# Two gathered tiles of rows in place of a combining pass that waits for the last two expert blocks

## The chip, the cores and the metric

One core of a Trainium2 chip runs the whole program once. The metric is the device time of one execution in microseconds; the kernel before has a median of 1506.51 us over 3 runs.

## The reference, cut to what matters

One decoder layer runs over 1056 tokens (1024 of a prompt and 32 of samples) of width 1024: a mixing sub-layer, then a mixture of 32 experts of which each token takes two, then a final RMSNorm. Only the end matters here:

```
h = x + mix
# expert e of token t, k = 0, 1:  silu(hn W_gate[e]) * (hn W_up[e]) W_down[e]
h[t] = h[t] + gate[t, 0] * out[t, 0] + gate[t, 1] * out[t, 1]
y = rms_norm(h, norm_final_w)
```

The reference sorts the 2112 assignments of a token to an expert by expert and pads them to blocks of 128 rows. With the given inputs no expert gets more than 110 rows, so there are 32 blocks, one for each expert. Block 30 holds 61 rows that are in use and block 31 holds 73; 121 tokens have a row in one of these two blocks, 13 of them in both.

## The kernel before, in words

The program is written engine by engine, and each engine runs its own list in the order in which it is written; semaphores join them. After the front part (projections, mixing, router) comes `experts`, and then `combine`, a block of its own that no engine enters before all have left `experts`.

**Experts.** Blocks are numbered 0 to 31. For each, POOL gathers the block's rows of the normalised input by an indirect DMA (`gather`, L1822 to L1828, tile `xg`), PE turns them (L1859), and ACT and DVE split all float32 operands into a high and a low part (`wgu_h` L1928, `wgu_l` L2048, `wd_h` L1934, `wd_l` L2057, `xh_blk` L1939, `xl_blk` L2052), so that PE makes each product of three matmuls (L62 to L64). SP loads the weights: four pieces of `wgu` (1 MB each, L1785) and four of `wd` (0.5 MB each, L1792) for each block, each as soon as DVE has read the piece before. The result of a block is copied by DVE to `yb` (`unload_y`, L2042) and POOL scatters its rows by an indirect DMA to the scratch tensor `picked` in HBM (`scatter`, L1830 to L1836). `picked` has 2112 rows: row t is the first expert's result of token t, row 1056 + t the second's. Rows of a block that are not in use have an index out of bounds and are not moved. Block 31 is different: its result goes to the tile `xg`, and POOL scatters it from there (L1846 to L1850). The last blocks stand behind the loops: `m` is 30 on SP, PE, ACT and DVE, and 29 on POOL.

At the end of its list for the experts SP loads the final norm's weights `w_final` (L1801), the residual rows of tiles 0 to 3 (`h_final`, L1804) and of tiles 4 to 8 (`h_late`, L1807), and then waits until all 32 scatters have landed:

```
            sp.wait_ge(y_stored, m * 16 + 32)
```

**Combine.** Tiles 0 to 7 are 128 tokens each and tile 8 is the 32 sample tokens. SP loads for each tile both rows of `picked` of each token (`yy`, 1 MB a tile, L2126). Tiles 8, 0, 2, 4 and 6 are summed by DVE (`add`, two SCALAR_TENSOR_TENSOR, L2186), tiles 1, 3, 5 and 7 by PE with matrices `diag` that hold the gates (L2148 to L2150). ACT takes the mean square and its root (L2165 to L2172), DVE takes the reciprocal and scales (`norm`, L2196 to L2204), and POOL stores the tile (L2134). The order is 8, 0, 1, ..., 7.

## Time and profile before

| | |
|---|---|
| median of 3 runs | 1506.51 us (1503.09 to 1506.59) |
| the profiled execution, its own time | 1505.11 us |
| its span in the trace | 1503.4 us |
| PE busy | 1416.1 us (94%) |
| DVE busy | 1061.5 us (71%) |
| ACT busy | 766.1 us (51%) |
| POOL busy | 568.4 us (38%) |
| data moved by the DMA engines | 361.07 MB |

The span begins with the first instruction and ends with the last; 1.7 us of the execution's own time lie outside of it. A busy share is an average over the whole program, in which the experts take from about 863 to 1464 us and combining from there to the end. In the profile's rows of waits, the time is what an engine sat idle before the instruction named, and behind the arrow stands what ended it.

### The profile page before, as it was taken

The page shows a single profiled execution, that of the slowest core. Times are in us where ns is not written, and L with a number is a line of the kernel's source. Part 1 is how long each engine was busy: PE and PEld are TensorE (multiplying, and loading weights), DVE is VectorE, ACT ScalarE, POOL GpSimd, SP SyncE. Part 2 cuts the span into 40 slices and gives each one's busy share as a digit, 9 for nine tenths or more (in the row PEclk, how much of TensorE's full clock was granted, in tenths as well). Part 3 has the DMA queues.
Part 4 walks back from the last instruction along what each step waited for, and adds up shares of the span by engine and source line. Part 5 has one row for each costly group of instructions (what it writes and reads, how often), then busy time and mean ns, then how long its engine had stood idle before and what let it go on. Part 6 is the DMA issues. An engine that isn't in the chain of part 4 may idle for free. (4 is left out here: it accounts for less than half of the span.)

```text
span 1503.4 us, 21686 instructions
## 1 busy us (share of the span) xinstructions
PE 1416.1 (94%) x7625; PEld 1233.0 (82%) x7625; DVE 1061.5 (71%) x1225; ACT 766.1 (51%) x891; POOL 568.4 (38%) x345
## 2 busy tenths in 40 slices
PE   6999999999999999899999659999999999999976
PEld 5999999999999998788877548888888888888852
DVE  6687722366666664545463579999999999999956
ACT  6332222333333335344433438777777777777734
POOL 2323324454444442485644014333433333333311
PEclk9999999999999999999999669999999999999997
DMA  5222333234444445876653659999999999999958
GB/s 197 65 78 86 126 95 111 80 130 143 144 141 147 138 144 167 294 219 239 209 168 130 231 201 383 402 396 390 377 381 362 389 379 383 385 388 387 369 211 343
DMA packets 115793, 361.07 MB, mean 240 GB/s; under 512 B 18772, under 2 KB 48468, under 8 KB 99348
## 3 DMA queue, kind: packets, MB, share of 16 engines
q1 hardware_dynamic: 100164, 322.37, 58.6%
q0 software_dynamic: 15568, 37.87, 7.3%
q8 instruction: 41, 0.67, 0.2%
q14 instruction: 20, 0.16, 0.0%
HBM read 316.52 MB, written 59.64 MB: 250 GB/s over the span
## 5 line engine op out<-in xcount | busy, mean ns | idle before, releaser
L2048 DVE TENSOR_TENSOR wgu_l<-wgu,wgu_h 128x2048 fp32r<-128x2048 f32 x128 | 290.0, 2288 | 27.4 <-ACT wgu_h L1928 26.5
L1928 ACT CAST wgu_h<-wgu 128x2048 fp32r<-128x2048 f32 x124 | 237.4, 1915 | 100.6 <-PE bank0and L64 100.5
L62 PE MATMUL bank0and<-wgu_h,xh_blk 128*128 128x512 f32 x512 | 203.7, 398 | 2.9 <-DVE xl_blk L2052 2.9
L64 PE MATMUL bank0and<-wgu_h,xl_blk 128*128 128x512 f32 x512 | 200.9, 392 | 0.0
L62 PE MATMUL bank0and<-xh,wh 128*128 128x352 f32 x576 | 197.6, 343 | 3.0 <-ACT raw L906 3.0
L63 PE MATMUL bank0and<-wgu_l,xh_blk 128*128 128x512 f32 x512 | 200.3, 391 | 0.0
L64 PE MATMUL bank0and<-xh,wl 128*128 128x352 f32 x576 | 186.7, 324 | 0.0
L63 PE MATMUL bank0and<-xl,wh 128*128 128x352 f32 x576 | 186.5, 324 | 0.0
L1671 POOL TENSOR_TENSOR wol<-wo,woh 128x1024 fp32r<-128x1024 f32 x48 | 121.4, 2536 | 123.5 <-ACT woh L996 123.5
L1835 POOL DMA_INDIRECT scratch_picked<-yb,dst x31 | 92.7, 2991 | 197.5 <-DVE yb L2042 197.5
L2057 DVE TENSOR_TENSOR wd_l<-wd,wd_h 128x1024 fp32r<-128x1024 f32 x128 | 148.2, 1219 | 1.2 <-ACT wd_h L1934 1.0
L1622 POOL TENSOR_TENSOR wl<-w,wh 128x1024 fp32r<-128x1024 f32 x36 | 87.7, 2437 | 155.7 <-ACT wh L893 155.7
L1934 ACT CAST wd_h<-wd 128x1024 fp32r<-128x1024 f32 x128 | 124.9, 1049 | 1.7 <-PE bank2and L64 1.7
L62 PEld LDWEIGHTS bank0and<-wgu_h,xh_blk 128*128 128x128 f32 x512 | 96.8, 189 | 22.7 <-issue 2.8
L62 PEld LDWEIGHTS bank0and<-xh,wh 128*128 128x128 f32 x576 | 109.7, 190 | 6.9 <-issue 5.6
L64 PEld LDWEIGHTS bank0and<-wgu_h,xl_blk 128*128 128x128 f32 x512 | 96.6, 189 | 20.8
L63 PEld LDWEIGHTS bank0and<-wgu_l,xh_blk 128*128 128x128 f32 x512 | 96.9, 189 | 19.4
L63 PEld LDWEIGHTS bank0and<-xl,wh 128*128 128x128 f32 x576 | 110.0, 191 | 2.6 <-issue 1.9
L64 PEld LDWEIGHTS bank0and<-xh,wl 128*128 128x128 f32 x576 | 109.3, 190 | 0.0
L1191 DVE COPY stage<-bank2and 128x512 f32<-128x512 f32 x26 | 18.0, 692 | 123.3 <-PE bank2and L568 123.3
L915 ACT ACTIVATE feat<-bank0and 128x352 f32<-128x352 f32 x48 | 22.1, 463 | 156.1 <-PE bank0and L64 156.0
L62 PE MATMUL bank2and<-wd_h,hT_h 128*128 128x512 f32 x248 | 99.3, 401 | 0.0
(496 smaller groups left out, 3234.5 us busy)
## 6 DMA issues: line engine op xcount, KB each, us to landing
wgu<-in_w_gate_up SPq DMA_DIRECT2D x128, 1024.0 KB, 7.6
wd<-in_w_down SPq DMA_DIRECT2D x128, 512.0 KB, 7.6
wo<-in_w_out SPq DMA_DIRECT2D x48, 512.0 KB, 4.9
w<-in_w_in_tiles SPq DMA_DIRECT2D x36, 512.0 KB, 3.6
yy<-scratch_picked SPq DMA_DIRECT2D x8, 1024.0 KB, 12.6
scratch_xb<-stage POOLq DMA_DIRECT2D x10, 512.0 KB, 4.0
xb<-scratch_xb SPq DMA_DIRECT2D x8, 640.0 KB, 4.4
scratch_uT<-feat SPq DMA_DIRECT2D x8, 528.0 KB, 5.0
```

What stands on the lines that cost most here:

```text
L62: nc.tensor.matmul(acc, lh, rh, start=start, stop=False)
L63: nc.tensor.matmul(acc, lh, rl, start=False, stop=False)
L64: return nc.tensor.matmul(acc, ll, rh, start=False, stop=stop)
L915: nc.scalar.activation(feat[q % 2][:, b * TB:(b + 1) * TB], bank[b][:, 0:TB], func).then_inc(acc_free, 1)
L1191: ins = nc.vector.tensor_copy(stage[j][:, 4 * g:4 * g + 4, :], bank[3 + g][:].rearrange("p (t c) -> p t c", t=4))
L1622: nc.gpsimd.tensor_tensor(wl[q % 2][:], w[q % 2][:], wh[q % 2][:].bitcast(F32), ALU.subtract).then_inc(w_split, 1)
L1671: nc.gpsimd.tensor_tensor(wol[n % 3][:], wo[n % 3][:], woh[n % 3][:].bitcast(F32), ALU.subtract).then_inc(w_split, 1)
L1835: pool.indirect_dma_start(out=S["picked"], out_offset=bass.IndirectOffsetOnAxis(ap=dst[:], axis=0), in_=yb[:], in_offset=None, bounds_chec ...
L1928: nc.scalar.copy(wgu_h[:, s], wgu[:, s]).then_inc(gu_high, 1)
L1934: nc.scalar.copy(wd_h[:, p, :], wd[:, p, :]).then_inc(down_high, 1)
L2048: nc.vector.tensor_tensor(wgu_l[:, s], wgu[:, s], wgu_h[:, s].bitcast(F32), ALU.subtract).then_inc(gu_split, 1)
L2057: nc.vector.tensor_tensor(wd_l[:, p, :], wd[:, p, :], wd_h[:, p, :].bitcast(F32), ALU.subtract).then_inc(down_split, 1)
```

## The change

The combining pass is moved into the block `experts`, and the function `combine` is gone.

- At the start of the experts SP stores the gates to a new scratch tensor `gates` and, behind the loads of block 1's `wgu`, loads `w_final` and the residual rows of tiles 0 to 3. Tiles 8 and 4 are loaded before the last `wd`, tiles 5, 6 and 7 behind it.
- POOL fills `yb` with zeros and scatters these zeros to the rows of blocks 30 and 31 in `picked`, between its first gathers.
- SP's wait before it loads `yy` has the same number, `m * 16 + 32`, but with the two scatters of zeros it is met when block 29 has been scattered. The nine tiles are then combined with zeros in the place of the rows of blocks 30 and 31, and SP, no longer POOL, stores them whole to one output `y`.
- POOL scatters block 30 only when all nine `yy` have been loaded, then block 31 when block 30 has landed. It then gathers two more tiles, 9 and 10: the residual rows, the gates, and both rows of `picked` of the tokens of block 30 and of block 31. DVE adds and scales them, and POOL scatters them to `y` when all nine stores have landed, tile 10 after tile 9 has landed.
- The tiles on PE are 2, 4, 6 and 7, the order is 8, 1, 0, 2, ..., 7, 9, 10.

```diff
+            for t in range(2):
+                rows, n = ((slice(0, SEQ), P), (slice(SEQ, T), TS))[t]
+                tiles = slice(0, NT) if t == 0 else slice(NT, NT + 1)
+                sp.dma_start(S["gates"][rows, :].rearrange("(t p) k -> p t k", p=n), S["gate"][0:n, tiles, :]).then_inc(loaded[0], 16)
             m = blocks_but_three(sp) + 1
             load_gate_up(1)
+            sp.wait_ge(rows_ready, 1)
+            sp.dma_start(w_final[:], A["norm_final_w"][0].partition_broadcast(P)).then_inc(loaded[0], 16)
+            for t in range(FIRST):
+                sp.dma_start(h[t], S["h"][t * P:t * P + P, :]).then_inc(loaded[t], 16)
...
+            sp.wait_ge(gu_split, m * 4 + 8)
+            sp.sem_inc(holder, 1)
+            load_h(NT)
+            load_h(4)
             load_down(m + 1)
...
+            for t in (5, 6, 7):
+                load_h(t)
+            picked = S["picked"].rearrange("(k t) d -> t k d", k=2)
             sp.wait_ge(y_stored, m * 16 + 32)
-            sp.sem_inc(holder, 1)
+            for t in (8, 1, 0, 2, 3, 4, 5, 6, 7):
+                used = 0 if t == 0 else (t + 1) // 2
+                if used:
+                    sp.wait_ge(gu_used, m * 4 + (4 + used))
+                sp.sem_inc(holder, 1)
+                sp.dma_start(yy[t][0:live(t)], picked[t * P:t * P + live(t)]).then_inc(loaded[t], 16)
+            for n, t in enumerate(ORDER[0:NT + 1]):
+                sp.wait_ge(out_ready, n + 1)
+                sp.dma_start(A["y"][t * P:t * P + live(t), :], h[t][0:live(t), :]).then_inc(out_stored, 16)
+            sp.wait_ge(out_stored, 16 * (NT + 1))
...
             gather(1)
+            for j in range(2):
+                if j:
+                    pool.wait_ge(y_stored, 16)
+                then_own(pool, nc.gpsimd.tensor_copy(dst[:], of_row[:, 1, bass.ds(m + (1 + j), 1)]), dst_ready, j + 1)
+                pool.indirect_dma_start(out=S["picked"], out_offset=bass.IndirectOffsetOnAxis(ap=dst[:], axis=0),
+                                        in_=yb[:], in_offset=None, bounds_check=2 * T - 1, oob_is_err=False).then_inc(y_stored, 16)
             gather(2)
...
+            is_loaded(pool, 0)
...
+            late_gather(0, h[NT + 1], S["h"])
+            for j in range(2):
+                late_gather(j, late_gate[:, j, :], S["gates"])
+            for t in range(NT + 1):
+                is_loaded(pool, t)
             scatter(m + 1)
...
+            pool.wait_ge(y_stored, m * 16 + 64)
             pool.wait_ge(y_done, last + 1)
...
+            pool.wait_ge(y_stored, m * 16 + 80)
+            pool.sem_inc(holder, 1)
+            for k in range(2):
+                late_gather(0, yy[NT + 1][:, k, :], S["picked"], k)
+            late_gather(1, h[NT + 2], S["h"])
+            for k in range(2):
+                late_gather(1, yy[NT + 2][:, k, :], S["picked"], k)
+            pool.wait_ge(out_stored, 16 * (NT + 1))
+            store_late(0)
+            pool.wait_ge(late_stored, 16)
+            store_late(1)
+            pool.wait_ge(late_stored, 32)
...
+            make_diag(0)
+            make_diag(1)
+            gated(m + 1)
+            low_down(m + 1, range(2))
+            low_hid(m + 1, (last_h, last_l))
+            dve.wait_ge(hid_ready, m + 2)
+            make_diag(2)
+            make_diag(3)
+            unload_y(m)
+            low_down(m + 1, range(2, 4))
             add(NT)
+            dve.wait_ge(down_used, (m + 1) * 4 + 4)
+            nc.vector.tensor_copy(xg[:], S["banks45"][:]).then_inc(y_done, 1)
+            add(1)
+            norm(NT)
             add(0)
...
+            norm(6)
+            norm(7)
+            dve.wait_ge(xg_loaded, m * 16 + 160)
+            dve.sem_inc(holder, 1)
+            add(9)
+            add(10)
+            norm(9)
+            norm(10)
```

The helpers that it calls are the ones that stood in `combine`, and these two on POOL:

```
            def late_gather(j, out, table, k=0):
                pool.indirect_dma_start(out=out, out_offset=None, in_=table,
                                        in_offset=bass.IndirectOffsetOnAxis(ap=late_row[:, j, k:k + 1], axis=0),
                                        bounds_check=(2 * T if k else T) - 1, oob_is_err=False).then_inc(xg_loaded, 16)

            def store_late(j):
                pool.wait_ge(out_ready, NT + 2 + j)
                pool.indirect_dma_start(out=A["y"], out_offset=bass.IndirectOffsetOnAxis(ap=late_row[:, j, 0:1], axis=0), in_=h[NT + 1 + j],
                                        in_offset=None, bounds_check=T - 1, oob_is_err=False).then_inc(late_stored, 16)
```

How it moves instructions: first SP at the end of the program, in the kernel before. `yy` with a number is the tile of one t, 10035 for t = 8 and 10027 on for t = 0 on; in square brackets stand the semaphores that the instruction waits for.

```order
L1807 DMA h_late<-scratch_h 128x1024 [waits gu_split]
L1807 DMA h_late<-scratch_h 128x1024 x3
L1807 DMA h_late<-scratch_h 32x1024
L1808 ISA
L1714 UNCONDITIONAL_BRANCH [waits y_stored]
L2122 UNCONDITIONAL_BRANCH [waits barrier_Pool_Activation_PE_DVE_SP_release]
L2126 DMA yy_10035<-scratch_picked 32x2x1024
L2126 DMA yy_10028<-scratch_picked 128x2x1024
L2126 DMA yy_10027<-scratch_picked 128x2x1024
```

The same place of the changed kernel, where `yy_8914` on are the tiles 0 on:

```order
L1844 DMA h_rest<-scratch_h 128x1024 x3
L1854 ISA
L1860 DMA yy_8922<-scratch_picked 32x2x1024 [waits y_stored,gu_used]
...
L1860 DMA yy_8920<-scratch_picked 128x2x1024 [waits gu_used]
L1860 DMA yy_8921<-scratch_picked 128x2x1024 [waits gu_used]
L1863 DMA out_y<-h_rest 32x1024 [waits out_ready]
L1863 DMA out_y<-h_first 128x1024 [waits out_ready] x4
L1863 DMA out_y<-h_rest 128x1024 [waits out_ready] x4
L1714 UNCONDITIONAL_BRANCH [waits out_stored]
```

The barrier between the two blocks is gone, the loads of `yy` follow a wait for `y_stored` directly, and the stores stand on SP's queue behind the loads.

POOL at the end of the program, in the kernel before:

```order
L1835 DMA scratch_picked<-yb,dst 2112x1024 [waits dst_ready,y_done]
L1846 ISA
L1846 COPY src<-of_row 128x1
L52 REGISTER_ALU
L1849 DMA scratch_picked<-xg,src 2112x1024 [waits dst_ready,y_done]
L1714 UNCONDITIONAL_BRANCH
L2128 UNCONDITIONAL_BRANCH [waits barrier_Pool_Activation_PE_DVE_SP_gather]
L2134 DMA out_y_sample<-h_late 32x1024 [waits out_ready]
```

And in the changed kernel, from block 30's scatter on:

```order
L1887 ISA [waits final_loaded5,final_loaded4,final_loaded6,final_loaded3,final_loaded7,final_loaded2,final_loaded1,final_loaded0]
L1889 COPY dst<-of_row 128x1 [waits y_stored]
L52 REGISTER_ALU
L1892 DMA scratch_picked<-yb,dst 2112x1024 [waits dst_ready,y_done]
...
L1938 DMA scratch_picked<-xg,src 2112x1024 [waits y_stored,y_done]
L1941 REGISTER_ALU [waits down_split]
L1917 DMA wd<-scratch_picked,late_row 128x1024 [waits y_stored]
L1917 DMA wd<-scratch_picked,late_row 128x1024
L1917 DMA xg<-scratch_h,late_row 128x1024
L1917 DMA wd<-scratch_picked,late_row 128x1024 x2
L1923 DMA out_y<-wgu,late_row 1056x1024 [waits out_ready,out_stored]
L1923 DMA out_y<-xg,late_row 1056x1024 [waits out_ready,late_stored]
```

Block 30's scatter has moved behind all loads of `yy`, and behind it stand five waits for a DMA one after the other: block 30's scatter, block 31's, the gathers (for which DVE waits), tile 9's store and tile 10's.

## Rows read from the trace of the kernel before

**Rows 1.** The page: span, and PE's busy time and share of the span

```profile
span 1503.4 us, 21686 instructions
PE 1416.1 (94%) x7625; PEld 1233.0 (82%) x7625; DVE 1061.5 (71%) x1225; ACT 766.1 (51%) x891; POOL 568.4 (38%) x345
```

**Rows 2.** Windows: stretch, its length, busy time by engine, TensorE's clock, DMA share, GB/s

```profile
900.00:1400.00 500.00, 498.88 (x2365) 414.90 (x2366) 480.30 (x340) 382.10 (x314) 181.81 (x112) 1.00 0.99 385
1440.35:1447.88 7.53, 7.53 (x37) 6.26 (x36) 1.61 (x2) 2.30 (x3) 0.00 (x2) 1.00 0.92 360
1458.05:1461.20 3.15, 0.00 (x0) 0.00 (x0) 0.00 (x0) 0.00 (x0) 0.97 (x1) 0.62 0.24 95
1470.50:1478.19 7.69, 7.57 (x12) 3.32 (x13) 6.52 (x6) 4.63 (x9) 0.52 (x1) 0.65 1.03 413
```

**Rows 3.** Timeline of SP's queue: start, us, line, issue, count

```profile
1434.14 3.71 SPq L1792 DMA_DIRECT2D wd<-in_w_down  x4
1437.90 0.98 SPq L1801 DMA_DIRECT2D w_final<-in_norm_final_w  x1
1441.21 2.77 SPq L1807 DMA_DIRECT2D h_late<-scratch_h  x5
1464.55 8.21 SPq L2126 DMA_DIRECT2D yy<-scratch_picked  x9
```

**Rows 4.** Timeline of POOL at the end; in square brackets idle before and its end

```profile
1439.36 0.99 POOL L1835 DMA_INDIRECT scratch_picked<-yb,dst  x1 [10.05 <-DVE yb L2042]
1447.88 0.34 POOL L1832 COPY dst<-of_row 128x1 int32 x1 [7.53 <-DMA scratch_picked<-yb,dst]
1458.05 0.97 POOL L1849 DMA_INDIRECT scratch_picked<-xg,src  x1 [4.10 <-DVE xg L2088]
1499.12 0.53 POOL L2134 DMA_DIRECT2D out_y_prompt<-h_late  x1 [0.99 <-DVE h_late L2200]
```

**Rows 5.** SP's waits from 1400 us on: the one for the scatters

```profile
SPq L1809 <- DMA scratch_picked<-xg,src: 17.2, 1, 17.2
```

**Rows 6.** Timeline of DVE while combining

```profile
1470.51 2.58 DVE L2186 SCALAR_TENSOR_TENSOR h_late<-yy,gate,h_late 32x1024 f32<-32x1024 f32 x2 [4.24 <-DMA yy<-scratch_picked]
1478.19 2.60 DVE L2186 SCALAR_TENSOR_TENSOR h_final<-yy,gate,h_final 128x1024 f32<-128x1024 f32 x2 [0.83 <-DMA yy<-scratch_picked]
1490.40 2.60 DVE L2186 SCALAR_TENSOR_TENSOR h_late<-yy,gate,h_late 128x1024 f32<-128x1024 f32 x2 [1.26 <-DMA yy<-scratch_picked]
1492.92 0.16 DVE L2196 RECIPROCAL st_f<-st_f 128x1 f32<-128x1 f32 x1
1493.11 1.29 DVE L2203 SCALAR_TENSOR_TENSOR h_late<-h_late,st_f,w_final 128x1024 f32<-128x1024 f32 x1
```

**Rows 7.** Timeline of SP, ACT and POOL at the start of the experts

```profile
878.21 26.15 SPq L1785 DMA_DIRECT2D wgu<-in_w_gate_up  x8
905.71 5.77 ACT L1928 CAST wgu_h<-wgu 128x2048 fp32r<-128x2048 f32 x3
882.89 1.05 POOL L1826 DMA_INDIRECT xg<-scratch_hn,src  x1 [2.64 <-PE bank4and L1859]
899.38 1.01 POOL L1826 DMA_INDIRECT xg<-scratch_hn,src  x1 [5.54 <-PE bank4and L1859]
```

**Rows 8.** Timeline of POOL: the first gather, then a scatter in the loop

```profile
875.59 1.11 POOL L1816 DMA_INDIRECT xg<-scratch_hn,of_row  x1 [11.57 <-DVE blk_i L2032]
880.05 0.20 POOL L1823 COPY src<-of_row 128x1 int32<-128x1 int32 x1 [3.35 <-DMA xg<-scratch_hn,of_row]
...
1209.10 2.83 POOL L1835 DMA_INDIRECT scratch_picked<-yb,dst  x1 [9.32 <-DVE yb L2042]
1218.77 1.53 POOL L1832 COPY dst<-of_row 128x1 int32 x1 [1.80 <-DMA scratch_picked<-yb,dst]
```

**Rows 9.** Timeline of ACT while combining: tile 6's square, sum and root

```profile
1493.03 1.06 ACT L2171 ACTIVATE junkf<-h_late 128x1024 f32<-128x1024 f32 x1 [2.68 <-DVE h_late L2186]
...
1494.22 0.30 ACT L2172 ACTIVATE st_f<-st_f,eps 128x1 f32<-128x1 f32 x1
```

More of the change, by code:

```diff
@@ L1763, in experts, with live, psum_of, is_loaded @@
         y_done, y_stored = sem("y_done"), sem("y_stored")
-        holder = C["holder"]
+        loaded = [sem(f"final_loaded{t}") for t in range(NT)]
+        loaded, loaded_at = loaded + [loaded[1]], [48 + 32, 64, 32, 32, 32, 32, 32, 32, 64]
+        out_stored, late_stored = sem("out_stored"), sem("late_stored")
+        summed, rms, out_ready = (sem(n) for n in ("summed", "rms", "out_ready"))
+        diag_ready, pe_summed = sem("diag_ready"), sem("pe_summed")
+        holder = C["holder"]
+        def live(t):
+            return TS if t == NT else P
+        def psum_of(t, half):
+            return bank[(0, 6, 2, 4)[ON_PE.index(t)] + half][:, :]
+        def is_loaded(eng, t):
+            eng.wait_ge(loaded[t], loaded_at[t])
         block = ctx.enter_context(nc.Block())
@@ L1918, in _ @@
             down(m + 1, first=4)
+            for n, t in enumerate(ON_PE):
+                is_loaded(pe, t)
+                if n == 0:
+                    pe.wait_ge(diag_ready, 8)
+                    pe.wait_ge(hT_done, m + 2)
+                if n >= 2:
+                    pe.wait_ge(y_done, m + (n - 1))
+                for half in range(2):
+                    s = slice(half * 512, (half + 1) * 512)
+                    acc = psum_of(t, half)
+                    nc.tensor.matmul(acc, C["ident"][:], h[t][:, s], start=True, stop=False)
+                    nc.tensor.matmul(acc, diag[n // 2][:, n % 2, 0, :], yy[t][:, 0, s], start=False, stop=False)
+                    nc.tensor.matmul(acc, diag[n // 2][:, n % 2, 1, :], yy[t][:, 1, s], start=False, stop=True).then_inc(pe_summed, 1)
         @block.scalar
@@ L2182, in add, with make_diag @@
+            def make_diag(n):
+                for k in range(2):
+                    nc.vector.tensor_scalar(diag[n // 2][:, n % 2, k, :], C["ident"][:], gate[ON_PE[n]][:, k:k + 1], None, ALU.mult).then_inc(diag_ready, 1)
             def add(t):
-                r = rows_of(t)
-                dve.wait_ge(loaded[t], loaded_at[t])
+                r = live(t)
+                if t <= NT:
+                    is_loaded(dve, t)
                 for k in range(2):
-                    ins = nc.vector.scalar_tensor_tensor(out=h[t][0:r, :], in0=yy[t][0:r, k, :], scalar=S["gate"][0:r, t, k:k + 1],
+                    ins = nc.vector.scalar_tensor_tensor(out=h[t][0:r, :], in0=yy[t][0:r, k, :], scalar=gate[t][0:r, k:k + 1],
@@ L2204, in norm @@
                                                          op0=ALU.mult, op1=ALU.mult)
                 ins.then_inc(out_ready, 1)
-            for n, t in enumerate(ON_PE):
-                for k in range(2):
-                    nc.vector.tensor_scalar(diag[:, n, k, :], C["ident"][:], S["gate"][:, t, k:k + 1], None, ALU.mult).then_inc(diag_ready, 1)
+            make_diag(0)
[3 more added lines that the diff above has]
+            low_hid(m + 1, (last_h, last_l))
@@ L2210, in _ @@
+            dve.wait_ge(hid_ready, m + 2)
[3 more added lines that the diff above has]
+            low_down(m + 1, range(2, 4))
             add(NT)
+            dve.wait_ge(down_used, (m + 1) * 4 + 4)
+            nc.vector.tensor_copy(xg[:], S["banks45"][:]).then_inc(y_done, 1)
+            add(1)
+            norm(NT)
             add(0)
-            norm(NT)
-            for t in range(2, NT, 2):
-                add(t)
-                norm(t - 2)
-                norm(t - 1)
@@ L2217, in _ @@
-            norm(NT - 2)
-            norm(NT - 1)
+            norm(1)
+            norm(0)
+            add(3)
+            norm(2)
+            norm(3)
+            add(5)
+            norm(4)
+            norm(5)
+            norm(6)
[6 more added lines that the diff above has]
+            norm(10)
+FIRST = 4
+ON_PE = [2, 4, 6, 7]
+ON_DVE = [8, 1, 0, 3, 5, 9, 10]
+ORDER = [8, 1, 0, 2, 3, 4, 5, 6, 7, 9, 10]
```

179 lines of the change are left out of this document (68 added, 111 removed).

## The prediction

> **What bounds the kernel now.** I read the windows first, then the queues at the end. In the loop over the experts PE is busy 498.9 of 500 us at the full clock, level 2.4 GHz, with the DMA engines at a share of 0.99 and 385 GB/s [rows 1, 2]. The change takes no matmul out of that loop, so a gain can only come from what follows it. There the timeline of SP is the one to read: the loads of `yy` begin at 1464.55 [rows 3], after SP has waited 17.2 us for block 31's scatter [rows 5]. That scatter starts at 1458.05 on POOL [rows 4]; SP's last issue of residual rows ends at 1443.98 [rows 3], and 17.2 us later is 1461.2. The other 3.3 us are the barrier and the entry into the next block of code. The last `yy` lands at 1490.4, when DVE stops waiting for it [rows 6]. From there 13.0 us of sums, norms and the last stores end the span at 1503.4. So the tail is: wait for the scatters (A), load 8.25 MiB (B), finish (C).
>
> The change starts B earlier, and puts a longer C behind it. I work out both.
>
> **A, when the loads of `yy` start.** SP now waits for block 29's scatter. It starts at 1439.36 and has landed at 1447.88, 7.5 us after its issue ended [rows 4], in a stretch where the DMA engines moved 360 GB/s [rows 2]. A scatter in the loop takes about as long: 1211.9 to 1218.8, 6.8 us [rows 8]. Block 31's scatter, with the DMA engines nearly empty, took 3.15 us from its start (1458.05 to 1461.2) [rows 2, 4]. These are the two prices, 1442.5 and 1447.9. In between lies what is queued on SP: `w_final` and tiles 0 to 3 no longer come here, and 4.3 MB remain (tiles 8 and 4 from 1432.8, `wd` from 1434.1 [rows 3], then tiles 5 to 7). At 413 GB/s [rows 2] these 10.5 us of transfer plus 2 us to the first landing run until about 1445.3. I take 1445.2, nearer to the loaded price because the queue is still full for most of it. There is no barrier any more, so the loads start 19.4 us earlier than at 1464.55.
>
> This is one place where the Trainium skill says otherwise. The trace shows a scatter landing 7.5 us after its issue beside a full queue of SP, against 2.2 us beside an empty one [rows 4]. By "DMA: Bandwidth & Descriptors", section "Queues, rings and completion order", each DMA engine goes round robin between the queues at every packet, so a scatter of 61 rows should hardly wait behind SP's backlog. By that A would be near 1442.5 and the total 2.7 us lower; the rows contradict it.
>
> **B, loading.** Before, tiles 8, 1, 0, 3 and 2 (4.25 MiB) had landed at 1478.19, 13.65 us after the first issue, without any store beside them until 1477.67, and tiles 8 and 1 at 1470.51, after 6.0 us [rows 6]: 3 MiB in 7.7 us, 2.55 us each, the 413 GB/s of that window [rows 2]. All nine thus need 13.65 + 4 x 2.55 = 23.9 us. Tile 9's residual rows are gathered meanwhile (61 rows of 4 KB, 0.6 us of transfer): 24.4 us, against 25.8 before, since the stores now queue behind the loads instead of beside them. All `yy` have landed at 1445.2 + 24.4 = 1469.6.
>
> **C, what follows the last `yy`.** The nine plain tiles are not what ends: DVE is through with the experts by 1458.05 [rows 4], add(8) fits ahead of that, and four adds at 2.60 and nine norms at about 1.5 [rows 6] make 24 us, until about 1482; ACT needs 1.5 us for a tile [rows 9] and runs beside. The stores then land by about 1486. What ends is POOL's list, one thing after the other:
> - Copy of the indices and wakes: 0.3 us.
> - Block 30's scatter: 1.0 us of issue [rows 4] and a landing between 2.2 and 7.5. SP's queue holds the stores of tiles 8, 1 and 0 by then (1.2 MB, 3 us at 413 GB/s) and gets 0.5 MB every 2 to 3 us afterwards, half of what the engines move. I take 3.5: 4.5 us.
> - Block 31's scatter, which now waits for block 30's: 1.0 + 3.0 = 4.0 us.
> - Five gathers: POOL issues one in 1.01 to 1.11 us [rows 7, 8], 5.2 in all, and the first gather of the program landed 3.35 us after its issue [rows 8]. With 0.5 us for an issue held up by DVE: 9.0 us. DVE waits for all five.
> - DVE: add(9), add(10), norm(9): 2.60 + 2.60 + 1.45 [rows 6] and a wake, 6.8 us. ACT's work for tile 9 lies beside add(10), tile 10's beside norm(9).
> - Store of tile 9, an indirect scatter of 61 rows at the empty price, 3.15 with a wake of 0.1; then tile 10's, which waits for it: 6.5 us.
> - To the span's end: before, the last store was issued at 1499.12 [rows 4]; with the same 3.0 us for its landing 1.2 remain.
>
> Sum 0.3 + 4.5 + 4.0 + 9.0 + 6.8 + 6.5 + 1.2 = 32.3 us, against 13.0 before. The span ends at 1469.6 + 32.3 = 1501.9, 1.5 us earlier than 1503.4. So the gain of 19.4 us at A and of 1.4 us in B is nearly all given back by 19.3 us in C.
>
> **The start of the experts** I cost at nothing. SP's 2.6 MB of `w_final` and residual rows enter at about 887, 6.4 us of transfer behind block 1's `wgu` (eight pieces of blocks 1 and 2 are issued from 878.2 to 904.4 [rows 7]). By DVE's timeline, which frees the place, block 2's first piece is issued near 894; it would land near 901; ACT first wants it at 905.71 [rows 7]. The cover is some 5 us; without it the cost is up to 6.4 us. The two scatters of zeros lie on POOL between the end of gather(1)'s issue at 883.9 and gather(2)'s issue at 899.4 [rows 7]: two issues of 1.0 to 2.83 and one loaded landing of 7.5, at most 14 of these 15.5 us. The store of the gates lies ahead of SP's wait for the tables. The two pairs of `diag` on DVE (1.7 us) fall into idle time or ahead of block 30's copy, which nobody waits for now.
>
> **Rivals.**
> - *The chain runs at the empty prices* (faster). Block 29's scatter lands after 3.15 us, loads start at 1442.5, all `yy` have landed at 1466.9, both scatters take 3.15. C is then 0.3 + 6.3 + 9.0 + 6.8 + 6.5 + 1.2 = 30.1, end 1497.0, 6.4 us earlier: 1500.1. For it: after 1470 the stores fill only half of the DMA engines. Against it: 7.5 us at 1440 [rows 4].
> - *The two scatters stand beside a full queue* (slower). SP's stores pile up behind the loads of `yy`, so block 30's and 31's scatters both land at the loaded 7.5 us: 0.3 + 8.5 + 8.5 + 9.0 + 6.8 + 6.5 + 1.2 = 40.8, end 1510.4, 7.0 us later: 1513.5. It becomes slower than before from 1.5 us of extra wait on, and by 0.3% from 6 us on, so both must be loaded. For it: every scatter in the loop and block 29's. Against it: DVE cannot make tiles faster than 0.5 MB in 2 us.
> - *DVE holds up POOL's indirect DMAs* (slower). A scatter's issue took 2.83 us under DVE's long subtractions and 0.97 with DVE idle [rows 4, 8]. Two scatters and the first two or three gathers fall into DVE's time until 1482, at 1.9 us each up to 9 us, less the 0.5 taken: end 1510, 1513 us. Against it: DVE's instructions here last 1.3 us, not 2.3, and those on PE's tiles read PSUM. The Trainium skill, "SBUF — State Buffer", has the rule: DVE with two SBUF inputs and a GpSimd instruction that reads SBUF exclude each other for a whole instruction. It speaks against this change, which puts eight such issues on the path.
> - *The added loads make PE wait at the start* (slower): up to 6.4 us, 1511.4. Or the tables of rows do not let SP go early, and nothing starts earlier: then C would come after the old B and the time would be near 1522; the code gives no sign of it.
>
> **The numbers.** The sum stands against the profiled execution: 1505.11 us of its own, span 1503.4. The median of the runs is 1506.51, 1.4 above. I take 1.5 off the median: **1505.0 us**. What a measurement can tell from no change is 0.3%, 4.5 us: 1502.0 to 1511.0 is "the same".
>
> My forecast has 0.57 (inside of the bound), the empty prices 0.22, full queue 0.10, DVE against POOL 0.06, loads at the start 0.05. The last three make slower 0.20, with a little of each side lost in the forecast's own spread. Faster by over 0.3% 0.23, within 0.57, slower 0.20. The range takes in the empty prices and reaches half-way into the slower cases: 1499.5 to 1512.0.
>
> **What would show it.** In the profile of the changed kernel: the first `yy` issue near 1445; the last landing near 1470; block 30's scatter issued right behind it and DVE idle for some 5 us before add(9), near 1487; tile 9's store near 1494; the loop unchanged, with PE at work on block 31's last matmul near 1456. If DVE has no idle time before add(9), the combining pass was the bound and not POOL's list. If PE's last expert matmul is late by over 1 us, the start was not free. If the two scatters take 8 us each, the full queue was right.

## The result, and the profile after

The changed kernel takes 1523.92 us, the median of 4 runs (1521.11 to 1525.09), against 1506.28 us of the kernel before: a ratio of 1.0119, 95% interval 1.0099 to 1.0139. It is slower by 17.6 us. The prediction was 1505.0 us with a range of 1499.5 to 1512.0: nearly no change was forecast, and the kernel became clearly slower. The profiled execution took 1523.35 us; its span is 1521.6 us, where the forecast of the span was 1501.9.

The page of the changed kernel, span and busy times, to be read beside [rows 1]:

```profile
span 1521.6 us, 21791 instructions
PE 1416.5 (93%) x7625; PEld 1233.7 (81%) x7625; DVE 1070.1 (70%) x1234; ACT 769.2 (51%) x897; POOL 574.9 (38%) x356
```

The engines have little more work: PE 0.4 us, ACT 3.1 us, DVE 8.6 us, POOL 6.5 us. The span has grown by 18.2 us, so most of the time is in waits. The timeline of SP's queue tells where the end of the program begins (start, us, line, issue, count), as [rows 3] did before:

```profile
1435.56 0.81 SPq L1844 DMA_DIRECT2D h_rest<-scratch_h  x2
1437.30 3.21 SPq L1827 DMA_DIRECT2D wd<-in_w_down  x4
1440.56 1.69 SPq L1844 DMA_DIRECT2D h_rest<-scratch_h  x3
1450.23 7.73 SPq L1860 DMA_DIRECT2D yy<-scratch_picked  x9
...
1464.47 0.35 SPq L1863 DMA_DIRECT2D out_y<-h_rest  x1
```

The loads of `yy` begin at 1450.23 instead of 1464.55: 14.3 us earlier, where 19.4 were forecast. The rest is in the timeline of POOL; it is the one to read from top to bottom, since each row waits for the one above it (in square brackets the idle time before, and what ended it), beside [rows 4]:

```profile
1441.98 0.99 POOL L1892 DMA_INDIRECT scratch_picked<-yb,dst  x1 [9.71 <-DVE yb L2180]
...
1476.62 0.18 POOL L1889 COPY dst<-of_row 128x1 int32 x1 [12.65 <-DMA yy<-scratch_picked]
1477.71 1.25 POOL L1892 DMA_INDIRECT scratch_picked<-yb,dst  x1 [0.91 <-POOL dst L1889]
...
1483.61 1.00 POOL L1938 DMA_INDIRECT scratch_picked<-xg,src  x1 [4.46 <-DMA scratch_picked<-yb,dst]
1488.85 1.03 POOL L1917 DMA_INDIRECT wd<-scratch_picked,late_row  x1 [4.24 <-issue]
...
1494.07 0.99 POOL L1917 DMA_INDIRECT wd<-scratch_picked,late_row  x1 [0.31 <-issue]
1507.07 1.59 POOL L1923 DMA_INDIRECT out_y<-wgu,late_row  x1 [12.01 <-DVE wgu L2247]
1511.70 0.98 POOL L1923 DMA_INDIRECT out_y<-xg,late_row  x1 [3.04 <-DMA out_y<-wgu,late_row]
```

The chain of work that ended last, followed back from the end, tells when the two scatters landed (start, us until the landing, what):

```profile
1477.71 5.00 DMA scratch_picked<-yb,dst
1483.61 4.02 DMA scratch_picked<-xg,src
```

So 0.9 us of the first 5.9 and 1.2 us of the next 5.2 lie between a landing and the start of the next issue. The last `yy` has landed at 1476.2 (at 1490.4 before). The span ends 45.4 us later; before it ended 13.0 us later. DVE's timeline in the same stretch, beside [rows 6]:

```profile
1485.56 1.41 DVE L2244 SCALAR_TENSOR_TENSOR h_rest<-bank4and,st_f,w_final 128x512 f32<-128x512 f32 x2
1499.63 2.61 DVE L2230 SCALAR_TENSOR_TENSOR wgu<-wd,late_gate,wgu 128x1024 f32<-128x1024 f32 x2 [12.66 <-DMA wd<-scratch_picked,late_row]
```

DVE is through with the nine plain tiles at 1487.0 and then idle for 12.7 us until the gathered rows are there. So POOL's list is the path, as forecast, and not the combining pass.

```profile
L1714 POOLq DRAIN  x1: 6492/6492/6492, 1457.8 to 1457.8; - x1
L1714 SPq DRAIN  x1: 7/7/7, 1461.4 to 1461.4; - x1
```

```profile
L1714 POOLq DRAIN  x1: 6274/6274/6274, 1515.1 to 1515.1; - x1
```

In the kernel before, SP was through at 1461.4, when block 31's scatter had landed, and POOL's DRAIN at 1464.3: this is what I had booked as "3.3 us of barrier and entry into the next block of code". At the end of the combining pass, a block of code in which POOL issues nine plain DMAs, the same instruction took 0.78 us:

```profile
L2099 POOLq DRAIN  x1: 784/784/784, 1502.4 to 1502.4; - x1
```

The change makes one block of code of the two. POOL's long DRAIN moves with it, from a place where it ended some 3 us behind the last scatter's landing to the very end, where nothing hides it.

### The profile page after: what moved, and what is told of

Read it like the earlier page. It is cut to its first block and busy times, and to the rows that moved or that the text cites. A ratio compares the mean times of both kernels' runs of the same rounds, so it can differ in the third digit from the quotient of the medians.

```text
span 1521.6 us, 21791 instructions
## 1 busy us (share of the span) xinstructions
PE 1416.5 (93%) x7625; PEld 1233.7 (81%) x7625; DVE 1070.1 (70%) x1234; ACT 769.2 (51%) x897; POOL 574.9 (38%) x356
## 5 line engine op out<-in xcount | busy, mean ns | idle before, releaser
L63 PEld LDWEIGHTS bank0and<-wgu_l,xh_blk 128*128 128x128 f32 x512 | 96.7, 189 | 19.3
```

Source lines behind the costliest of these rows:

```text
L63: nc.tensor.matmul(acc, lh, rl, start=False, stop=False)
```

## The experiments

Two theories for the 45.4 us. **A**: POOL's list is a chain of links that add up, and the DRAIN at its end is a link of its own, 6.3 us. **B**: the chain is long because its DMAs wait for one another or for SP's queue, and the DRAIN is only the shadow of the last landing. Several kernels were measured once. The kernel before spread from 1502.1 to 1507.6 us over 21 executions, so single runs are judged here by the links in their traces, not by their times.

### The DRAIN, moved into idle time

```diff
                 late_gather(j, late_gate[:, j, :], S["gates"])
+            nc.gpsimd.drain()
             for t in range(NT + 1):
                 is_loaded(pool, t)
```

> Edit: one more DRAIN on POOL, after the first three late gathers and ahead of its wait for the yy, where POOL idles for 12 us. Theory A (POOL's DRAIN at the end of a block of code takes time for each indirect DMA issued since the last one; 64 of them in the kernel before, 75 here): the added DRAIN takes 5 to 7 us in the idle time, the one at the end falls from 6.3 to below 1.5 us, and the span falls by 5 us to about 1517. Theory B (a DRAIN takes 6.3 us whenever the last DMA of POOL was an indirect one): both take 6 us and the span stays at 1521 to 1522.

Measured: 1516.27 us (1 run), span 1513.7. POOL's two DRAINs, first the one at the end and then the added one:

```profile
L1714 POOLq DRAIN  x1: 788/788/788, 1512.7 to 1512.7; - x1
```

```profile
L1931 POOLq DRAIN  x1: 10227/10227/10227, 1458.0 to 1458.0; - x1
```

The one at the end fell from 6274 to 788 ns, with the same last store ahead of it: theory A is right on the DRAIN, worth 5.5 us. The added one ends at 1468.2 and so lies in time in which POOL waits for the last `yy` anyway. It is longer than expected: 7.2 us from the end of POOL's last issue, at 1461.0. The other 2.4 us of the 7.9 between the spans are not its doing: block 29's scatter starts 2.9 us earlier in this execution (1439.07).

### The wait between the two last scatters taken out

```diff
             then_own(pool, nc.gpsimd.tensor_copy(src[:], of_row[:, 1, bass.ds(last, 1)]), dst_ready, last + 3)
-            pool.wait_ge(y_stored, m * 16 + 64)
             pool.wait_ge(y_done, last + 1)
```

> Edit: block 31's scatter doesn't wait until block 30's has landed. Main theory (each link of POOL's chain costs its landing plus about 1 us of waking and issue): the five gathers start 4 to 4.5 us earlier after the last yy, near 1484.5, and the span falls by as much, to about 1517.5. Rival (the landing is set by the stores that fill the DMA engines, and two scatters beside each other take as long as one after the other): the span stays above 1520.

Measured: 1521.34 us (1 run), span 1519.5. POOL's timeline:

```profile
1476.23 0.46 POOL L1889 COPY dst<-of_row 128x1 int32 x1 [12.33 <-DMA yy<-scratch_picked]
1477.60 1.28 POOL L1892 DMA_INDIRECT scratch_picked<-yb,dst  x1 [0.91 <-POOL dst L1889]
1479.98 1.89 POOL L1937 DMA_INDIRECT scratch_picked<-xg,src  x1 [0.91 <-POOL src L1934]
1486.87 1.03 POOL L1917 DMA_INDIRECT wd<-scratch_picked,late_row  x1 [4.99 <-DMA scratch_picked<-xg,src]
```

The second scatter is issued 3.6 us earlier, but from the copy to the first gather it takes 10.6 us against 12.2: 1.6 us, not the 4 or more of the expectation. Between the kernel of the first experiment and the next one below, both with the DRAIN moved, the same stretch shrinks by 0.7 us only (12.6 to 11.9). Two scatters side by side land hardly sooner than one after the other, so the wait that the change adds here costs little. The same edit with the DRAIN moved as well:

> Edit: the changed kernel with the added DRAIN on POOL and without the wait between block 30's and 31's scatter. Main theory (both are links of one chain, so their gains add): 5.2 + 1.6 = 6.8 us less than the changed kernel, a span near 1514.5 where the loop slips as in its profile, and still some 10 us slower than the kernel before.

Measured: 1514.48 us, median of 4 runs, ratio to the kernel before 1.0058 (1.0042 to 1.0074); span 1513.0. The medians differ by 9.4 us. The traces explain less of it: from the start of block 29's scatter to the end of the span it is 73.6 us instead of 79.6, so the two edits give 6.0 us there, near the 6.8 expected, and 2.5 us are an earlier scatter in this execution. The rest of the difference between the medians stays unexplained. Either way it is not enough to be level with the kernel before.

### SP's queue in front of block 29's scatter

The residual rows of tiles 5 to 7 go behind the fourth load of `yy`, so that less stands in SP's queue when the scatter is issued:

```diff
             load_down(m + 1)
-            for t in (5, 6, 7):
-                load_h(t)
...
                 sp.dma_start(yy[t][0:live(t)], picked[t * P:t * P + live(t)]).then_inc(loaded[t], 16)
+                if t == 2:
+                    for later in (5, 6, 7):
+                        load_h(later)
```

> Edit: the changed kernel with the residual rows of tiles 5, 6 and 7 loaded behind the yy of tile 2 and not ahead of SP's wait for block 29's scatter. Theory A (a scatter lands late as long as SP's queue is full): the queue is empty by about 1445.5, and the scatter lands 4 to 5 us after its start instead of 8.2, so the loads of yy begin 3 to 4 us earlier; the last yy lands at the same time as before, since the 1.6 MB are then moved among them. Theory B (the landing doesn't depend on the queue's length): 8 us from its start to the first yy, and the last yy lands 4 us later.

Measured: 1522.69 us (1 run), span 1520.3. POOL's scatter, SP's first `yy`, and the window between them (length, busy time by engine, TensorE's clock, DMA share, GB/s):

```profile
1439.59 0.99 POOL L1893 DMA_INDIRECT scratch_picked<-yb,dst  x1 [9.77 <-DVE yb L2181]
1445.18 1.96 SPq L1858 DMA_DIRECT2D yy<-scratch_picked  x4
```

```profile
1444.00:1446.00 2.00, 2.00 (x10) 1.65 (x10) 0.57 (x1) 0.60 (x1) 0.00 (x0) 1.00 0.10 39
```

From the scatter's start to the first `yy` it is 5.6 us. With the queue left as it was it took 8.25 us in the changed kernel and 7.9 to 8.9 us in six others, so the scatter waits for what stands in SP's queue, and less of it means an earlier landing. The last `yy` gains nothing: POOL's next copy starts 35.6 us after the scatter, against 34.6 in the changed kernel, since the moved rows are now loaded between the others. So the start of the loads can be bought earlier, but in this way not their end.

### The loads at the start of the experts

In one kernel `w_final` and the rows of tiles 0 to 3 are loaded ahead of block 1's `wgu`, in the other at their old place behind the last `wd`:

```diff
+            sp.dma_start(w_final[:], A["norm_final_w"][0].partition_broadcast(P)).then_inc(loaded[0], 16)
+            for t in (2, 3):
+                sp.dma_start(h[t], S["h"][t * P:t * P + P, :]).then_inc(loaded[t], 16)
+            sp.wait_ge(rows_ready, 1)
+            for t in (0, 1):
+                sp.dma_start(h[t], S["h"][t * P:t * P + P, :]).then_inc(loaded[t], 16)
             m = blocks_but_three(sp) + 1
             load_gate_up(1)
-            sp.wait_ge(rows_ready, 1)
...
```

```diff
             load_gate_up(1)
-            sp.wait_ge(rows_ready, 1)
-            sp.dma_start(w_final[:], A["norm_final_w"][0].partition_broadcast(P)).then_inc(loaded[0], 16)
-            for t in range(FIRST):
-                sp.dma_start(h[t], S["h"][t * P:t * P + P, :]).then_inc(loaded[t], 16)
...
             load_down(m + 1)
+            sp.wait_ge(rows_ready, 1)
+            sp.dma_start(w_final[:], A["norm_final_w"][0].partition_broadcast(P)).then_inc(loaded[0], 16)
...
```

> Edit: the loads of w_final and of the residual rows of tiles 0 to 3 are issued before block 1's wgu (w_final and tiles 2 and 3 at once, tiles 0 and 1 when the tables of rows are ready), not behind it. Main theory (the loss is spread over three places: 2.8 us in the loop by these loads, 4 us ahead of the last yy, 13 us in POOL's list and its exit): ACT no longer waits for wgu in blocks 2 and 3, block 29's scatter starts near 1439.3 instead of 1441.98, and the span falls by 2 to 3 us, to about 1519. Rival (the scatters of zeros and the late gather of block 2 slow the start): block 29's scatter stays at 1442, span 1521 to 1522.

> Edit: the same five loads stand where the kernel before had them, behind the last wd. Main theory: the loop is as fast as before (block 29's scatter starts at 1439.4), but 2.6 MB more are queued on SP when that scatter is issued, so it lands no earlier after its issue than before (7.5 us) and the loads of yy, queued behind residual rows that are still being moved, take about 28 us instead of 26. Span 1519 to 1522. Rival (the place of these loads doesn't matter for the loop): block 29's scatter at 1442 and a span of 1524 or more.

Measured: 1521.96 us with the loads ahead (span 1520.2), 1529.44 us with them at their old place (span 1527.4), 1 run each. The loop is best measured from POOL's first gather to ACT's first operation on block 31's product. Of the kernel before and of the changed one:

```profile
1444.51 0.60 ACT L1944 ACTIVATE act_g<-bank0and 128x512 f32<-128x512 f32 x1 [9.74 <-PE bank0and L64]
```

```profile
875.54 1.11 POOL L1872 DMA_INDIRECT xg<-scratch_hn,of_row  x1 [11.35 <-DVE of_row L2170]
...
1447.11 0.60 ACT L2059 ACTIVATE act_g<-bank0and 128x512 f32<-128x512 f32 x1 [9.74 <-PE bank0and L64]
```

With the first gather at 875.59 before [rows 8] that is 568.9 us before and 571.6 us after: 2.6 us. With the loads at their old place it is 568.4. But the 2.6 us are not one price that the loads have. In five executions with the loads at their old place, of the kernel before and others, the loop took 568.4 to 569.0; with the loads where the change has them it took 571.6 in this one, 569.5 to 569.8 in five others and 567.9 in one. The trace of the changed kernel shows how such a loss comes about: ACT waiting for block 2's weights, later PE waiting for gathered rows, then a stretch in which the granted clock of TensorE was 0.51, its lower level of 1.2 GHz:

```profile
908.75 1.92 ACT L2043 CAST wgu_h<-wgu 128x2048 fp32r<-128x2048 f32 x1 [1.52 <-DMA wgu<-in_w_gate_up]
949.24 1.72 PE L1961 MATMUL bank4and<-ident,xg 128*128 128x128 f32 x8 [1.99 <-DMA xg<-scratch_hn,src]
950.50:953.00 2.50, 2.50 (x9) 2.02 (x8) 1.15 (x2) 2.01 (x2) 1.04 (x1) 0.51 1.03 424
```

Block 1's product comes 1.6 us later than before, counted from the first gather, and by block 3 that is made up. Block 4's then comes 21.6 us behind block 3's, where it was 18.6, and the loop doesn't make that up. With the loads ahead of block 1's the loop takes 571.6 again, where I had expected a gain: there the first block's product comes 25.4 us after the first gather instead of 22.3.

The kernel with the old place is the slowest of all, because everything that leaves the start comes back at the end. SP's loads of `yy`, beside [rows 3]:

```profile
1448.22 14.59 SPq L1860 DMA_DIRECT2D yy<-scratch_picked  x9
```

The nine issues take 14.6 us instead of 7.7 and the last `yy` lands at about 1481.5. The span is 5.8 us longer than with the loads at the start, although the loop is 3.2 us shorter, and not the 1519 to 1522 us that I had expected. Of the change's parts the early place is one that pays, as far as one run each can tell.

### The new order without the blocks put off

The changed kernel, but SP waits for all 32 scatters again, tiles 9 and 10 are left out with their gathers and stores, and the loads stand at their old place; the scatters of zeros are left out too. One block of code, tile order and stores on SP stay.

```diff
-ON_DVE = [8, 1, 0, 3, 5, 9, 10]
-ORDER = [8, 1, 0, 2, 3, 4, 5, 6, 7, 9, 10]
+ON_DVE = [8, 1, 0, 3, 5]
+ORDER = [8, 1, 0, 2, 3, 4, 5, 6, 7]
```

> Edit: the changed kernel without the scatters of zeros and without tiles 9 and 10; SP waits for all 32 scatters, then loads yy; w_final and tiles 0 to 3 are loaded where the kernel before had them. It keeps the single block of code and SP's stores. Main theory (the late tiles and their chain are the loss, the single block itself is a gain): yy from 1461.5 on, all landed near 1486.5, POOL's DRAIN falls into the loads, last store near 1498, and the span ends near 1500, 3 us less than before. Rival (the stores behind the loads on SP's queue, or the order of the tiles, cost something): 1503 or more.

Measured: 1505.05 us, median of 11 runs, ratio 0.9996 (0.9986 to 1.0005): no change. POOL's last scatter, SP's loads, and POOL's DRAIN:

```profile
1459.57 0.97 POOL L1901 DMA_INDIRECT scratch_picked<-xg,src  x1 [3.01 <-DVE xg L2212]
1462.85 8.20 SPq L1856 DMA_DIRECT2D yy<-scratch_picked  x9
```

```profile
L1714 POOLq DRAIN  x1: 6489/6489/6489, 1459.3 to 1459.3; - x1
```

From the scatter's start to the first `yy` 3.3 us, against 6.5 before: one block of code hides the DRAIN beside the combining pass. But 39.65 us follow from there to the end, against 38.85, since tiles 6 and 7 both go to PE and DVE has to wait for the second:

```profile
1497.76 0.16 DVE L2190 RECIPROCAL st_f<-st_f 128x1 f32<-128x1 f32 x1 [3.40 <-ACT st_f L2051]
```

That eats 0.8 of the 3.2 us. In this execution the last scatter is also 1.5 us later than before's, 1.2 us of it already at the first gather. I had expected a span near 1500 us and had not counted the wait for ACT. Why so little of the other 2.4 us shows in the medians stays open.

### The DRAIN in the kernel before

If the DRAIN is what stands between the last scatter and the loads, the kernel before can have its gain in one line:

```diff
             scatter(m)
+            nc.gpsimd.drain()
             scatter(m + 1)
```

> Edit, to the kernel before: one DRAIN on POOL between block 29's and block 30's scatter, where it idles for 7.5 us. Theory (a DRAIN costs POOL some 0.1 us for each DMA issued since the last one): the DRAIN at the end of the experts, which ran from 1457.8 to 1464.3 and held up the barrier 3 us beyond the landing of block 31's scatter, ends with that landing; the loads of yy start near 1461.5 instead of 1464.55, and the kernel is 2.5 to 3 us faster than before, ratio 0.998. Rival (the barrier waits for something else): no change.

Measured: 1501.24 us, median of 10 runs, ratio to the kernel before 0.997 (0.996 to 0.998). Beside [rows 3, 4]:

```profile
1456.27 0.97 POOL L1850 DMA_INDIRECT scratch_picked<-xg,src  x1 [4.10 <-DVE xg L2089]
1459.84 8.13 SPq L2127 DMA_DIRECT2D yy<-scratch_picked  x9
```

```profile
L1714 POOLq DRAIN  x1: 3573/3573/3573, 1456.0 to 1456.0; - x1
```

From the scatter to the first `yy` 3.6 us instead of 6.5: the end of the experts is now the scatter's own landing. The trace accounts for 2.9 us; the medians differ by 4.7, and the interval reaches from 3 to 6. This is the fastest version of the study, faster than both kernels.

On top of it, norm(4) goes ahead of add(6) on DVE, which fills the 1.9 us for which DVE waits there for the last `yy`:

> The kernel before with a DRAIN on POOL ahead of block 31's scatter (the fastest run so far, 0.997 of the kernel before), and with DVE's order changed in the combining pass: norm(4) ahead of add(6), so that it fills the 1.3 to 1.9 us in which DVE is idle for the last yy. Theory A (after the last yy only DVE's list counts, and this norm leaves it): 1.2 to 1.5 us less than the run with the DRAIN alone, ratio to the kernel before 0.9955 to 0.9965, that is 1499.5 to 1500.5. Theory B (another engine takes over: ACT's part of tile 4 or the matmuls of tiles 6 and 7 come later by it): ratio stays at 0.997, with DVE waiting for ACT or PE at the last norms as in the run with one block put off.

Measured: 1502.30 us, median of 6 runs, ratio 0.9971 (0.9959 to 0.9983). In the profile the time from the first `yy` to the end fell from 39.4 to 38.1 us, but the measurement doesn't tell it from the version above, so it stays open whether it is worth anything.

### What the design could give

Two kernels take the waits of blocks 30 and 31 apart. In both, the DRAIN stands ahead of the wait for the plain tiles' stores, the two blocks are scattered to a tensor of their own as soon as their rows are written, and the late gathers read the first tensor; tiles 9 and 10 thus leave out the results of blocks 30 and 31.

```diff
-            for t in range(NT + 1):
-                is_loaded(pool, t)
-            scatter(m + 1)
+            scatter(m + 1, S["apart"])
...
-            pool.indirect_dma_start(out=S["picked"], out_offset=bass.IndirectOffsetOnAxis(ap=src[:], axis=0),
+            pool.indirect_dma_start(out=S["apart"], out_offset=bass.IndirectOffsetOnAxis(ap=src[:], axis=0),
...
+            nc.gpsimd.drain()
             pool.wait_ge(out_stored, 16 * (NT + 1))
```

> The changed kernel with the DRAIN put where POOL is idle, and with blocks 30 and 31 scattered to a tensor of their own as soon as their rows are written, beside the loads of yy and without waiting for them. The gathers of the last rows still read the first tensor, so tiles 9 and 10 leave out what blocks 30 and 31 compute (part of the result is missing from the output). It asks for the most that the design could give if the two scatters did not have to wait for the last yy. Theory A (POOL's list is a sum of links: wake, issue, landing, and each link that is taken out of it is a gain of its own length): the two scatters (some 10 us from the index copy to the first gather) leave the path; 0.5 MB or so of scattered rows go beside yy, so that the last yy lands 1 to 3 us later; the first gather starts about 1479 to 1481, the five land about 1490, DVE is then free at once, tile 9's store is issued near 1496 to 1498, tile 10's 4.6 us later, and the span ends near 1503 to 1506: level with the kernel before, about 10 us below the run with the DRAIN alone (1513.7). Theory B (the combining pass on DVE is the bound as soon as POOL's list is short): DVE is done with nine tiles at 1486.97 plus 1 to 3 us, so its idle time before add(9) is below 2 us and the gain is cut to about 8 us or less.

In the second, the gathers don't wait for those scatters either; the wait stands behind the DRAIN, ahead of the stores:

```diff
             pool.wait_ge(down_split, m * 4 + 12)
-            pool.wait_ge(y_stored, m * 16 + 80)
```

> As the run before it, with the last rows' five gathers no longer waiting for the landing of blocks 30's and 31's scatters (the tensor that they read isn't the one that those write; tiles 9 and 10 again leave out what blocks 30 and 31 compute, so part of the result is missing). This is POOL's list without either scatter's landing in front of the gathers. Theory A (POOL's list is the path and a sum): the gathers are issued from about 1476.5 on, right behind block 31's scatter, to 1483; beside the last loads of yy they land 5 to 7.5 us later, 1488 to 1490; DVE is done with nine tiles at 1487 to 1489, so that its idle time before add(9) falls from 7.9 to under 2 us; then 7.5 us to tile 9's store and 8.2 to the last landing: the span ends at 1504 to 1506, level with the kernel before (1503.4). Theory B (traffic beside the loads of yy only moves the delay: the yy land later by what the gathers take): the last yy lands 2 us or more later, DVE's nine tiles end at 1490 or later and the span ends above 1507.

Measured: 1513.44 us (span 1511.7) and 1509.73 us (span 1508.0), 1 run each. POOL's timeline of the first, then of the second:

```profile
1465.41 1.27 POOL L1892 DMA_INDIRECT scratch_apart<-yb,dst  x1 [0.91 <-POOL dst L1889]
...
1474.83 1.58 POOL L1936 DMA_INDIRECT scratch_apart<-xg,src  x1 [7.54 <-DMA scratch_apart<-yb,dst]
1483.80 1.03 POOL L1917 DMA_INDIRECT wd<-scratch_picked,late_row  x1 [7.39 <-DMA scratch_apart<-xg,src]
...
1503.22 1.58 POOL L1923 DMA_INDIRECT out_y<-wgu,late_row  x1 [13.18 <-DVE wgu L2246]
```

```profile
1472.82 1.27 POOL L1917 DMA_INDIRECT wd<-scratch_picked,late_row  x1 [0.30 <-issue]
...
1478.30 1.30 POOL L1917 DMA_INDIRECT wd<-scratch_picked,late_row  x1 [0.30 <-issue]
1499.52 1.58 POOL L1923 DMA_INDIRECT out_y<-wgu,late_row  x1 [19.92 <-DVE wgu L2247]
```

Beside the loads of `yy` each scatter takes 9.4 and 9.0 us to the next instruction, against 6.1 and 4.4 in the run with the DRAIN alone: of the 10.7 us by which block 30's scatter starts earlier 7.9 are lost to the full queue, and the first gather is only 2.8 us earlier. In the second kernel the gathers are issued from 1472.82 to 1479.6 and DVE can start only at 1492.07, 12.5 us after the last issue; in the changed kernel it was 4.6 us after it (1495.06 to 1499.63). In the first kernel DVE was still idle for 7.94 us before add(9), so the pass on DVE is not the bound, but the span missed theory A's 1503 to 1506 by 6 us. The second ended above the 1507 that theory B had named, though not by its mechanism: DVE was through with the nine tiles at 1486.7, not at 1490 or later, and then waited 5.4 us for the gathers. Theory A had the path right and the landing of the gathers wrong, 1491.9 and not 1488 to 1490. In these single runs, even with neither scatter in front of the gathers and with the DRAIN hidden, the design ends 4.6 us behind the kernel before, and its 1509.73 us lie above all 21 executions of that kernel.

## Why the prediction was wrong

The direction of the argument held: the loads start earlier, and POOL's list gives the time back. The terms of the sum were too small, nearly all of them on the same side. **The step that failed** is the sum for C: 32.3 us where 45.4 were measured, so that 14.3 us were won and 32.4 given back, where 19.4 and 19.3 were forecast. The largest single error in it is its last term, 1.2 us to the span's end where the DRAIN made 6.5. Forecast span 1501.9, measured 1521.6: 19.7 us, of which A has 5.0, B 1.6 and C 13.1.

**A, the first load: 1450.23, not 1445.2.** 2.6 us are the loop, whose start I "cost at nothing"; as a rival it had 0.05. The cover of some 5 us held for block 2's first piece, and ACT waited 1.5 and 1.4 us for the next two. That it came to 2.6 us is partly this execution's luck, since six others with the same loads lost 0.9 us at most. The other 2.4 are the scatter: I let SP's queue be empty by 1445.3, and took 5.8 us from the scatter's start; it took 8.25. The loaded price of 8.5 us stood in [rows 4] and was the right one. The Trainium skill's "DMA: Bandwidth & Descriptors", section "Queues, rings and completion order", says that each DMA engine takes the queues in turn at every packet; by that, SP's backlog should hardly matter. The kernel with less in SP's queue landed its scatter 2.65 us sooner, and the one with 2.6 MB more in it took 9.3 us, so here it matters.

**B, loading: 26.0 us, not 24.4.** The reason given, that stores queue behind the loads instead of beside them, was wrong. SP issues the first store at 1464.47, and stores and loads share the engines from then on. The nine tiles took 25.9 us in the kernel before, 26.3 with the DRAIN moved and 26.4 in the kernel before with an added DRAIN: nothing that the change does moves this term.

**C, from the last `yy` to the end: 45.4 us, not 32.3.** By the links of the list:

| link | forecast | measured |
|---|---|---|
| wake, index copy, to the scatter's start | 0.3 | 1.5 |
| block 30's scatter | 4.5 | 5.9 |
| block 31's scatter | 4.0 | 5.2 |
| five gathers, to DVE's start | 9.0 | 10.8 |
| add(9), add(10), norm(9), to the store's start | 6.8 | 7.4 |
| stores of tiles 9 and 10 | 6.5 | 8.0 |
| to the span's end | 1.2 | 6.5 |

The last row is the largest miss: "to the span's end, 1.2". I took it from the kernel before, whose POOL had issued nine DMAs since its last DRAIN, and read the long DRAIN in the middle of that kernel as a barrier of 3.3 us which the change removes. It doesn't remove it; it moves it to the end. The experiment that put it back into idle time took 5.5 us off. With that term right the forecast would still have been 14 us short. The other six rows miss 7.7 us together, and most of that is one mistake: I took an issue and a landing from rows, and left out what stands between two of them. The trace shows 0.91 us from an index copy to the DMA that uses it, 0.30 us between two gathers, and 0.8 to 1.2 us from a landing to the next issue. The landings themselves were nearly right: 5.0 and 4.0 us from the start of a scatter, against 4.5 and 4.0.

**The rivals.** "The empty prices": no, the two scatters took 5.9 and 5.2 us against 3.15. "Beside a full queue": half; they lie between 3.15 and 8.5, and only the kernels that put them beside the loads of `yy` had 8.4 to 9.4. "DVE holds up POOL": hardly, since DVE was idle during all but two of the nine issues. These seven took 0.98 to 1.03 us; the two that ran beside DVE's work took 1.25 (block 30's scatter) and 1.59 (tile 9's store). The Trainium skill's rule in "SBUF — State Buffer", section "SBUF: two separate sides", is that DVE and a GpSimd instruction can exclude each other; the longer of the two ran beside a DVE operation with both inputs in SBUF and fits it, but no run tests it, and the two rows cost 0.9 us together, not 9. "Loads at the start": 2.6 us in this execution, mostly under 1. "Nothing starts earlier", for which a time near 1522 was named, has nearly the measured number by accident: the loads did start 14.3 us earlier. The point named as the test, DVE idle before add(9), came out on the side of POOL's list, with 12.7 us instead of 5.

**The range** reached half-way into the slower cases. Each of them was priced with the other terms at my own values; that several terms could be too small together was in none of them, and the DRAIN was in no case at all.

## What to carry to other kernels

Where work moves out of a block of code, or two blocks become one, look at the DRAINs of the sequencers too: they are in no engine's busy time, and a POOL that has issued many DMAs can be held up for microseconds at the next one, so give it one where POOL is idle anyway. A chain of dependent indirect DMAs costs per link a wake and an issue beside the landing; price it from start to start of a link in a trace, and give a link the price of the queue that stands beside it. A part of the work that is put off to start something earlier has to be short when it comes back: here 14.3 us were won and 32.4 paid.

## What the runs showed of the hardware

**POOL's DRAIN grows with the DMAs that POOL has issued since the one before; in the last part of the program by about 82 ns for each.** The counts are those of the lists in the code. Two DMAs (the two stores, in the kernels with a tensor apart):

```profile
L1714 POOLq DRAIN  x1: 212/212/212, 1511.3 to 1511.3; - x1
```

Nine gave 784 and 788 ns, whether nine plain stores or nine indirect ones; 76 gave 6274 ns (32 gathers, 32 scatters, 2 of zeros, 8 late gathers, 2 stores). From 2 to 9 that is 82 ns each, from 9 to 76 again 82 ns each. For the 64 of the kernel before this makes 5.3 us, counted from the end of the last issue, 1459.0, to 1464.3, where its DRAIN does end. This is a rule fitted to these few rows; no run varied the number alone, and one row speaks against it. In the front part of the kernel before, POOL issues 56 plain DMAs, the last at 578 us, and its DRAIN there is short of the 4.6 us that the rule asks for:

```profile
L132 POOLq DRAIN  x1: 3777/3777/3777, 825.2 to 825.2; - x1
```

It starts with POOL's last operation, which itself takes 2.3 us. So the size for another program has to be read from its trace. With a DMA still under way the DRAIN lasts at least until it has landed: 3573 ns in the kernel with the added DRAIN, where one scatter is out. Beside the loads it lasts longer still: the added DRAINs ended 7.2 us (in the first experiment) to 15.4 us (in the last) after POOL's last issue ahead of them, in the last one some 3 us after the gathered rows had reached DVE.

**An indirect DMA is slow beside a full queue, and several side by side don't help.** From issue to the next instruction a scatter took 3.6 us with the DMA engines nearly empty, 4.4 to 6.8 beside stores, and 8.4 to 9.4 beside the loads of `yy`. Two at once took 10.6 and 11.9 us up to the first gather, where two in a row took 12.2 and 12.6. Five gathers beside loads and stores landed 12.5 us after the last issue, and 4.6 us after it when issued later. Why it is so much more than its bytes stays open.
